# Second attention of both layers: value product one slot later, fills in two passes, keys doubled by DMA

## What is computed

```
s_nb  = q . k_window * scale + bias      # 8 heads, head dim 64, latent queries
s_ctx = q . k_context * scale
p     = softmax([s_nb, s_ctx])
out   = p_nb . v_window + p_ctx . v_context
# context queries (layer 0 only): softmax(q . k_context * scale) . v_context
```

## Time and profile before

| | us |
|---|---|
| median of 3 runs (lowest, highest) | 2425.41 (2423.21, 2426.27) |
| profiled execution: own time | 2428.46 |
| profiled execution: span | 2426.2 |
| second attention, layer 0 | about 514 to 692 |
| second attention, layer 1 | about 1792 to 1930 |

### The profile page before, as it was taken

The page is one execution under the profiler, slowest core; times in us unless marked ns, Lnnn a source line. Parts: engine busy times, 40 slices in busy tenths (PEclk is TensorE's granted clock), DMA queues, the critical chain, the costliest instruction groups (busy, mean ns, idle before and its releaser), DMA issues.

```text
span 2426.2 us, 34451 instructions
## 1 busy us (share of the span) xinstructions
PE 2292.5 (94%) x13082; PEld 2093.1 (86%) x13082; DVE 1195.2 (49%) x2401; ACT 947.6 (39%) x1850; POOL 1090.1 (45%) x844
## 2 busy tenths in 40 slices
PE   8999899998899999999999989899988899999997
PEld 4899888987799999999999878778877789888887
DVE  6979666435542355653821263556535525212124
ACT  4232566335532651111121254266435537422223
POOL 1434455334433554433533443446434457644545
PEclk9999999999999999999999999999999999999999
DMA  6624100211113545443421542211212246422335
GB/s 256 236 93 147 62 27 27 64 63 51 54 56 112 169 139 200 138 145 115 161 82 61 165 142 88 78 44 36 77 58 73 62 148 193 146 95 95 113 114 181
DMA packets 118798, 264.90 MB, mean 109 GB/s; under 512 B 13444, under 2 KB 13700, under 8 KB 117256
## 3 DMA queue, kind: packets, MB, share of 16 engines
q1 hardware_dynamic: 109728, 238.08, 29.6%
q10 hardware_dynamic: 8936, 25.04, 3.1%
HBM read 252.58 MB, written 10.49 MB: 108 GB/s over the span
## 4 chain that ended last, share of the span: by engine, by line
PE 78%; DVE 12%; ACT 4%; issue 2%; DMA 1%; POOL 1%; ACTq 0%; SPq 0%; DVEq 0%
PE ps L1843 29%; PE ps L1845 13%; PE ps L1855 13%; PE ps L1956 6%; PE ps L2220 6%; PE ps L2184 4%; PE ps L2165 2%; DVE pt_lo L1588 2%; PE ps L2134 1%; PE ps L2030 1%; DVE max_c L1571 1%; DVE ps L1563 1%; DVE ada_unused_gate_up L1144 1%; DVE max_c L1560 1%; POOL p_sb L568 1%
## 5 line engine op out<-in xcount | busy, mean ns | idle before, releaser
L556 POOL TENSOR_TENSOR w_lo<-raw,w_hi 128x512 fp32r<-128x512 f32 x632 | 866.3, 1394 | 970.7 <-ACT w_hi L630 970.3
L630 ACT ACTIVATE w_hi<-raw 128x512 fp32r<-128x512 f32 x632 | 367.0, 627 | 686.4 <-PE ps L1845 246.2
L568 POOL TENSOR_TENSOR p_sb<-p_sb,row_inv 128x768 f32<-128x768 f32 (+2 forms) x160 | 185.5, 1170 | 302.3 <-DVE row_inv L1581 301.7
L1843 PE MATMUL ps<-h_hi,w_lo 128*128 128x384 f32 (+1 forms) x832 | 300.6, 361 | 0.0
L1843 PE MATMUL ps<-h_lo,w_hi 128*128 128x384 f32 (+1 forms) x832 | 300.4, 361 | 0.0
L1843 PE MATMUL ps<-h_hi,w_hi 128*128 128x384 f32 (+1 forms) x832 | 300.4, 361 | 0.0
L1671 DVE TENSOR_TENSOR ps<-silu_g,ps 128x768 f32<-128x768 f32 (+3 forms) x52 | 37.8, 726 | 376.7 <-PE ps L1845 177.9
L1843 PEld LDWEIGHTS ps<-h_hi,w_hi 128*128 128x128 f32 x832 | 156.2, 188 | 16.0
L1843 PEld LDWEIGHTS ps<-h_lo,w_hi 128*128 128x128 f32 x832 | 156.2, 188 | 15.9
L1843 PEld LDWEIGHTS ps<-h_hi,w_lo 128*128 128x128 f32 x832 | 156.2, 188 | 15.8
L2220 PE MATMUL ps<-h_hi,w_lo 128*128 128x384 f32 (+1 forms) x408 | 136.8, 371 | 27.2 <-DVE k_ll L1528 14.9
(11 more groups left out here) (248 smaller groups left out, 5491.5 us busy)
## 6 DMA issues: line engine op xcount, KB each, us to landing
raw<-in_stream SPq DMA_DIRECT2D x632, 256.0 KB, 2.8
ada_raw_gate_up<-in_w_ada SPq DMA_DIRECT2D x48, 512.0 KB, 3.5
bias_sb<-in_bias ACTq DMA_DIRECT2D x32, 320.0 KB, 2.8
ada_raw_tokens_a<-in_w_ada SPq DMA_DIRECT2D x16, 512.0 KB, 3.6
ada_raw_merge_c<-in_w_ada SPq DMA_DIRECT2D x16, 512.0 KB, 3.5
scratch<-xr ACTq DMA_DIRECT2D x16, 512.0 KB, 4.2
xr<-scratch SPq DMA_DIRECT2D x14, 512.0 KB, 4.7
first_raw<-in_w_first SPq DMA_DIRECT2D x5, 1024.0 KB, 14.1
```

What stands on the lines that cost most here:

```text
L556: nc.gpsimd.tensor_tensor(w_lo[:, u % 2, cols], raw[:, u % 2, cols], w_hi[:, u % 2, cols].bitcast(F32), ALU.subtract).then_inc(S("lo_made" ...
L568: nc.gpsimd.tensor_tensor(p, p, row_inv[:, c:c + 1].broadcast_to([P, keys]), ALU.mult).then_inc(S("p_ready"), 1)
L630: nc.scalar.activation(w_hi[:, s, cols], raw[:, s, cols], ACT.Copy).then_inc(S("hi_made"), 1)
L1843: last = nc.tensor.matmul(bank(0), tile, x[:, k, 0:split], start=start, stop=stop)
```

## The change

- PE, second attention only (`shifted`): slot n is now `score(n+1)`, all of `attend(n-1)`, half the fill, `turn` groups 0 and 1, the other half, `turn` group 2; one `attend` stands after the loop.
- A 768-wide fill is made in two passes over the 24 steps (`fill_passes`): columns 0 to 383, then 384 to 767. Passes of the second attention alternate between banks 6 and 7 (`pass_bank`), and a pass waits only for the last but one (`held`). Each pass is evacuated by itself by ACT and DVE.
- ACT and DVE have a slot order of their own (`late_slot`): ACT first requests the bias row, evacuates a pass, then makes both `probs(n+1)` with `move_half` between them, then `turned_hi`; DVE makes both `maximum(n+1)` first, then `invert` and `fold`, the rests, and all `turned_lo` last. POOL makes both `normalise` before `o_rest`.
- `key_copies` issues two DMAs from ACT's queue instead of two ACT instructions.

The first attention computes what it did, in the same order.

POOL, `attention`:

```diff
                         normalise(n + 1, 0)
+                        if shifted(ph):
+                            normalise(n + 1, 1)
```

ACT, `key_copies`:

```diff
-                    last = nc.scalar.activation(k_hh[1][HD * (1 - x):HD * (2 - x), n, :],
-                                                k_hh[1][HD * x:HD * x + HD, n, :].bitcast(F32), ACT.Copy)
-                last.then_inc(S("k_dup"), 1)
+                    act.dma_start(k_hh[1][HD * (1 - x):HD * (2 - x), n, :].bitcast(F32), k_hh[1][HD * x:HD * x + HD, n, :].bitcast(F32)).then_inc(S("k_dup"), 16)
```

ACT, the new slot:

```diff
+                def late_slot(n, f, groups):
+
+                    h, j = divmod(n, pairs)
+                    if j < 2 and h + 1 < HEADS:
+                        load_bias(ph, h + 1, j)
+                    early, late = (first_pass_ended(ph, n, late) for late in (False, True))
+                    if f is not None:
+                        fill_out(f, len(fill_passes(ph, f)) - 1)
+                    if early is not None:
+                        fill_out(early, 0)
+                    if n + 1 < count:
+                        probs(n + 1, 0)
+                    if n:
+                        move_half(n - 1)
+                    if n + 1 < count:
+                        probs(n + 1, 1)
+                    for g in groups[:2]:
+                        turned_hi(n, g)
+                    if f is not None:
+                        act.wait_ge(S("unit_done"), ph.unit + f + 1)
+                        split(ph.unit + f + 2, f % 2)
+                        if f < 6 and f % 2:
+                            key_copies(f // 2 + 1, at(ph, "fill_out") + passes_to(ph, f + 1))
+                    if n and (n - 1) // pairs % 2:
+                        out_hi(n - 1)
+                    if late is not None:
+                        fill_out(late, 0)
+                    for g in groups[2:]:
+                        turned_hi(n, g)
```

DVE, the new slot:

```diff
+                def late_slot(n, f, groups):
+
+                    early = first_pass_ended(ph, n, False)
+                    late = first_pass_ended(ph, n - 1, True) if n else None
+                    if n + 1 < count:
+                        maximum(n + 1, 0)
+                        maximum(n + 1, 1)
+                        invert(n + 1, 0)
+                    if n:
+                        fold(n - 1)
+                    if n + 1 < count:
+                        invert(n + 1, 1)
+                    if late is not None:
+                        fill_rest(late, 0)
+                    if f is not None:
+                        fill_rest(f, len(fill_passes(ph, f)) - 1)
+                    if early is not None:
+                        fill_rest(early, 0)
+                    for g in groups:
+                        turned_lo(n, g)
```

PE, the wait of a pass in `fill`:

```diff
-                            if f or half:
+                            held = 2 if branch == 1 else 1
+                            if m >= held:
 
-                                pe.wait_ge(S("fill_out"), at(ph, "fill_out") + fill_halves(ph) * f + half)
+                                pe.wait_ge(S("fill_out"), at(ph, "fill_out") + m - held + 1)
                                 if branch == 1:
-                                    pe.wait_ge(S("fill_lo"), at(ph, "fill_lo") + min(f, 6))
+                                    pe.wait_ge(S("fill_lo"), at(ph, "fill_lo") + min(m - held + 1, passes_to(ph, 6)))
```

PE, the new slot:

```diff
+                    if shifted(ph):
+                        if n:
+                            attend(n - 1, range(len(turn_groups(branch, (n - 1) % pairs))))
+                        fill(n, 0)
+                        for g in groups[:2]:
+                            turn(n, g)
+                        fill(n, 1)
+                        for g in groups[2:]:
+                            turn(n, g)
+                        continue
```

The passes and their banks:

```diff
+def fill_passes(ph, f):
+
+    if ph.tiles > LT or ph.part and f < 6 and f % 2:
+        return ((0, HALF), (HALF, TOK))
+    return ((0, LAT),)
+
+
+def pass_bank(ph, f, i):
+
+    return FILL_BANK[ph.part] + (passes_to(ph, f) + i) % 2 if ph.part else FILL_BANK[0]
```

More of the change, by code:

```diff
@@ L990, in attention @@
                     if f is not None:
[L991 removed]
+                        fill_out(f, len(fill_passes(ph, f)) - 1)
+                    early, late = (first_pass_ended(ph, n, late) if branch == 1 else None for late in (False, True))
+                    if early is not None:
+                        fill_out(early, 0)
                     turned_hi(n, 0)
@@ L1518, in query_rest, with key_rest @@
                     q = q_st[1][c][x]
-                    last = nc.vector.scalar_tensor_tensor(halves(q[other, 0:w], w), product(qk_bank(c, 0), w, rows), QSCALE,
-                                                          halves(q[rows, 0:w].bitcast(F32), w), ALU.mult, ALU.subtract)
+                    last = nc.vector.scalar_tensor_tensor(halves(q[other, a:b], w), product(bank, w, rows), QSCALE,
+                                                          halves(q[rows, a:b].bitcast(F32), w), ALU.mult, ALU.subtract)
                 last.then_inc(S("fill_lo"), 1)
-            def key_rest(c, filled):
+            def key_rest(c, bank, a, b, filled):
+                w = b - a
                 dve.wait_ge(S("fill_out"), filled)
@@ L1527, in key_rest @@
                     rows, n = slice(HD * x, HD * x + HD), 2 * (c % 2) + x
-                    last = nc.vector.tensor_tensor(halves(k_ll[1][rows, n, :], TOK), product(qk_bank(c, 1), TOK, rows),
-                                                   halves(k_hh[1][rows, n, :].bitcast(F32), TOK), ALU.subtract)
+                    last = nc.vector.tensor_tensor(halves(k_ll[1][rows, n, a:b], w), product(bank, w, rows),
+                                                   halves(k_hh[1][rows, n, a:b].bitcast(F32), w), ALU.subtract)
                 last.then_inc(S("fill_lo"), 1)
@@ L2212, in fill @@
                                 pe.wait_ge(S("values_lo"), at(ph, "values_lo") - ALLT + 2)
-                        if branch == 0:
-                            wide = ph.width > LAT
-                            runs = ((7, HALF * half, HALF * half + HALF) if wide else (7, 0, LAT),)
-                        else:
-                            wide = (TOK if f < 6 and f % 2 else ph.width) > LAT
-                            runs = ((6, 0, HALF), (7, HALF, TOK)) if wide else ((6, 0, LAT),)
-                        for bank, a, b in runs:
-                            last = nc.tensor.matmul(ps[:, bank, 0:b - a], tile, x[:, k, a:b], start=r == 0, stop=r == FILL_STEPS - 1,
-                                                    skip_group_check=True)
+                        last = nc.tensor.matmul(ps[:, bank, 0:b - a], w[:, u % 2, k * P:(k + 1) * P], x[:, k, a:b], start=r == 0,
+                                                stop=r == FILL_STEPS - 1, skip_group_check=True)
                         if r == FILL_STEPS - 1:
-                            last.then_inc(S("fill_half" if half < fill_halves(ph) - 1 else "unit_done"), 1)
+                            last.then_inc(S("fill_half" if i < len(passes) - 1 else "unit_done"), 1)
                 if branch == 0:
@@ L2263, in attention @@
                     attend(n, groups[2:])
+                if shifted(ph):
+                    attend(count - 1, groups)
             def bridge(ph):
@@ L2463, in turn_order, with shifted, passes_to, first_pass_ended @@
     return {name: i for i, name in enumerate(names)}
-def fill_halves(ph):
-    return 2 if ph.part == 0 and ph.tiles > LT else 1
-def fill_steps(ph, n):
-    pairs = ph.tiles // 2
-    each = FILL_STEPS * fill_halves(ph) // pairs
-    return range((n + 2) * each, (n + 3) * each) if n + 2 < FILLS * pairs else range(0)
+def shifted(ph):
+    return ph.part == 1
+def fill_passes(ph, f):
+    if ph.tiles > LT or ph.part and f < 6 and f % 2:
+        return ((0, HALF), (HALF, TOK))
+    return ((0, LAT),)
+def passes_to(ph, f):
+    return sum(len(fill_passes(ph, n)) for n in range(f))
+def pass_bank(ph, f, i):
+    return FILL_BANK[ph.part] + (passes_to(ph, f) + i) % 2 if ph.part else FILL_BANK[0]
+def fill_steps(ph, n):
+    f, part = divmod(n + 2, ph.tiles // 2)
+    steps = FILL_STEPS * len(fill_passes(ph, f))
+    return f, range(steps * part // (ph.tiles // 2), steps * (part + 1) // (ph.tiles // 2)) if f < FILLS else range(0)
+def first_pass_ended(ph, n, late):
+    f, part = divmod(n + 2, ph.tiles // 2)
+    if part == 1 and f < FILLS and len(fill_passes(ph, f)) == 2 and late == (ph.tiles > LT):
+        return f
+    return 0 if n == 0 and not late and len(fill_passes(ph, 0)) == 2 else None
 def fill_ended(ph, n):
```

115 lines of the change are left out of this document (60 added, 55 removed).

## The result

| | before | after |
|---|---|---|
| median, us | 2425.84 (2423.21 to 2426.44) | 2387.28 (2385.95 to 2388.41) |
| ratio | | 0.9843 (95% interval 0.9826 to 0.9860) |
| span of the profiled execution, us | 2426.2 | 2386.6 |
| layer 0, start of slot 0 to start of slot 22 | 158.5 | 134.4 |
| layer 1, start of slot 0 to start of slot 14 | 122.1 | 103.3 |

The change is 38.6 us faster; the forecast was 30.4 us, 2395. The time lies inside the range, 2377 to 2414.

What follows compares the result with a forecast made beforehand. PE in the second attentions was taken as held by DVE's rests, maxima and `pt_lo`; 17.4 us less in layer 0 and 13.0 in layer 1 make 30.4, hence 2398.1 profiled, 2395 median; range 2377 to 2414.

Steps and rivals of the forecast that it cites:

- What bounds it: Second attentions: no engine full; DVE's rests, maxima and `pt_lo` stand inside PE's slots, 7.2 and 8.7 us each.
- The loop DVE - ACT - DVE: Maxima, exponentials, `pt_hi`, `pt_lo`: 5.9 us a slot, over PE's 5.35 in layer 0's j = 0.
- Doubled keys by DMA: Six key slots: DMAs follow the split, scores wait some 3.6 us, slots take 9.3 and 9.8 us.
- The landing: Key-doubling DMAs of 192 KB, SBUF to SBUF: 2.8 us each, taken from the bias row.
- The clock behind the stops: Lower PE clock after six key stops: 0.5 us added in layer 0, 1 us in layer 1, each.
- The last slots: Slots without a fill, bound from scores to `pt_lo` in both orders: counted equal.
- The passes: Two passes in alternating banks: 2.76 us stalls go, no PE cost, ACT's rests add about 0.3 us a fill.
- Bias rows first: ACT's bias request moved earlier in the slot: worth nothing measurable, keeps shorter slots from waiting.
- A: Rival: DVE-ACT-PE loop tighter than laid out, gain only 10 to 16 us, 2410 to 2416; chance 0.18.
- B: Rival: doubled-key copies hide, key slots 7.0 to 7.6 us, 18 us more gain, 2377; beyond 45 us chance 0.07.
- C: Rival: key DMAs land slowly; at 8.0 us, 31 us lost and the whole gain gone; chance 0.07.
- D: Rival: passes still wait for banks, PE stops 1 to 2 us at 14 evacuations, 2420 to 2426; chance 0.06.

Runs made afterwards that it cites:

- e2: Changed kernel with the two key-doubling DMAs issued right behind the evacuation of the key's second pass, ahead of the exponentials; 2374.92 us, ratio 0.9780.
- e1: Changed kernel with one wait more: the key-doubling DMAs are issued only once both halves of the split are written; 2403.23 us, ratio 0.9905.
- e4: Changed kernel with the old slot order on all engines, keeping two passes in alternating banks and the DMA; 2423.72 us, ratio 0.9990.
- e8: Changed kernel (new order, DMA, bias first) with the 768-wide fill in one pass over both banks as before; 2450.39 us, ratio 1.0089.
- e6: Changed kernel with the bias row requested last in a slot, as before, instead of first; 2402.85 us, ratio 0.9902.
- e7: As e2, but the keys are doubled by ACT's two Copy instructions instead of two DMAs; 2377.11 us, ratio 0.9793.
- e3: Changed kernel with the keys doubled by two ACT Copy instructions at the same place, behind the split, instead of DMAs; 2384.21 us, ratio 0.9832.

## Why the prediction was right, and where its size was off

**What bounds it** held. PE was held by DVE's rests and by `pt_lo`; with both out of the way the slots are what PE needs. In layer 0 5.6 and 5.65 us were forecast for j = 1 and j = 2 and 5.45 and 5.56 measured, 6.3 for j = 0 and 6.02 to 6.16 measured. In layer 1 a slot under a key fill takes 7.40 us (forecast 7.6), a gate slot 6.01 (6.3), and the three under a query fill 7.5, of which 1.5 is the clock behind a stop: e2 has 6.0 there (forecast 6.15). The loop DVE - ACT - DVE, laid out at 5.9, binds where it was said to, in the j = 0 slots of layer 0: all six waits of transposes for `pt_lo` in the counted slots, 4.2 us, are there, and the two j = 0 slots without an evacuation take 5.30. Apart from key slots and the clock behind them, the slots are 7 us shorter in all than laid out.

**The failing step** is in "Doubled keys by DMA": "the split at 6.0, the DMAs land at 8.8 and 9.15". The first DMA left at 4.33 us into the slot, the second at 4.83, not at 6.0, and the scores could start at 7.9. A stop is 2.0 to 2.2 us instead of 3.6, a key slot 7.9 and 8.45 instead of 9.3 and 9.8: 8.4 us for the six. e1 shows it by putting the missing wait in: the DMAs leave 5.9 us into the slot, and the stops are 3.8 us. The trace of before had it already, in the slot of the earlier trace rows:

```profile
602.94 0.34 ACTq L745 DMA_DIRECT2D bias_sb<-in_bias  x1
```

That is the bias row's request, and it begins ahead of the split at 603.12 and the copies at 604.31, which stand before it in ACT's program. I had read such a row's duration and not its place.

**The landing** was right: 2.8 us median for the 192 KB, as taken from the bias row. The Trainium skill, DMA: Bandwidth & Descriptors, section "Anatomy of one DMA — SWDGE (gpsimd) path", has figures for another issuing engine, from which the estimate was 2.45 us; the trace does not agree, and the row after decides for 2.8:

```profile
k_hh<-k_hh ACTq DMA_DIRECT2D x16, 192.0 KB, 2.8
```

**The clock behind the stops** was priced too low: 0.5 and 1 us, 4.5 us in all. Where it fell, the slot behind cost 1.5 us more (7.06 and 7.08 instead of 5.56 in layer 0, about 7.5 instead of 6.0 in layer 1); it fell behind five of the six stops, 7.5 us. The windows around a stop after which it fell and one after which it did not (the two numbers ahead of the last two: granted clock and DMA share):

```profile
554.50:558.50 4.00, 3.91 (x19) 3.94 (x20) 2.20 (x9) 0.78 (x2) 2.00 (x3) 0.57 0.41 131
...
592.70:598.00 5.30, 5.27 (x37) 5.27 (x38) 3.07 (x12) 2.97 (x8) 3.63 (x4) 1.00 0.33 99
```

The first is mostly the lower of TensorE's two levels, 1.2 GHz, the second 2.4. Both follow a stop of 2.2 us; why they differ is open.

**The last slots** were counted as equal and are not: from the scores that open slot 22 to the first merge product, layer 0 took 682.02 to 689.61, 7.6 us, and takes 657.98 to 667.81, 9.8 us. PE has nothing to fill in there, waits for `pt_lo`, and works at a granted clock of 0.50 from 664 to 668. With 1.4 us more between the two attentions and small ends that is 3.3 us of loss which the forecast did not have.

**The sum of the errors.** 8.4 (key slots) + 7.1 (other slots) - 3.0 (clock) - 3.3 (outside the counted slots) = 9.2 us; the spans' difference, 39.6, stands 9.2 above the 30.4. The two losses, 6.3 us together, hid part of a gain that the forecast had also put too low.

**The passes**, "no cost" for PE and 0.3 us a fill for DVE and ACT, hold: two rests take 1.12 us a pass (588.30). What the forecast did not see is how the two parts hang together: it counted 17 and 13 us for both at once, so the sum was right, but each part alone gives next to nothing or a loss (e4, e8). **Bias rows first**: "worth nothing measurable, and it keeps shorter slots from waiting". The second half is right, and so the first is wrong: without it the kernel loses 15.6 us (e6).

**The rivals.** A (loop tighter) did not come. Its sign, plain slots near 7 us, is met in number by the three query slots of layer 1 at 7.5, but that is the clock behind the stops (granted 0.77 from 1796.6 to 1804.1), and e2 has 6.0. B (the copies hide, 2377) is what e2 does on purpose, at 2374.9: its price was near (key slots of 7.0 to 7.6, measured 6.70 and 7.10), its condition was not met by the change. C (slow copies) fell with the landing of 2.8 us. D (the stall moves to the banks) did not come in this kernel; a moved stall is what e4 and e8 show, each with one of the two parts missing.

## What to carry to other kernels

An edit that lets work be late (more buffers, smaller passes) and an edit that makes it late (a new order) have to be priced together and built together; tried one at a time here, one gave nothing and the other lost 1%. When a copy is moved to a DMA, put its issue right behind the instruction that produces the data, and on a queue whose engine nobody waits for. Most of the gain here was the place: the early place brought 12 us with the DMA (e2) and 7 with ACT's own copies (e7 against e3), and the DMA itself nothing at the late place and 2 to 3 us at the early one. SP's queue brought a few more, and what stood behind it there, the weights, paid for part of it. A transfer that hid in a long slot has to be looked at again as soon as slots get shorter.

## What was not expected of the hardware

- DMA instructions on ACT's queue do not keep their place among its computing instructions. In after the first of the two left 0.41 us before the start of a split written ahead of it, and 0.56 us after the start of the `pt_hi` written ahead of that. If it must not, it needs a wait on what the earlier instruction gives.
- A DMA of 64 partitions from SBUF to SBUF held ACT's queue for 0.47 and 0.61 us, a bias row of 128 partitions from memory for 0.33. A pair costs 1.13 us of ACT, two thirds of the 1.70 us that the copies themselves take there.
- Six stops of 2.1 us cost more than their own length: with them out the granted clock was 1.00 throughout both attentions, and that alone gave 7.6 us in the slots behind; the key slots themselves gave 7.5, because issuing the DMAs early cost 5.2 of the stops' 12.7.
